# Expert retrieval in a two-layer trunk: second-table rows gathered per token and summed in four column groups, one tile behind the first table

## The reference

```python
top_s, pos = lax.top_k(cand, P_TOPK)
eidx = jnp.take_along_axis(cand_idx, pos, axis=-1)
gate = jax.nn.softmax(top_s, axis=-1).astype(xc.dtype)
u = jnp.take(u_tab, eidx, axis=0)
act = jax.nn.gelu(jnp.einsum('thkd,td->thk', u, xc))
vv = jnp.take(v_tab, eidx, axis=0)
return jnp.einsum('thk,thkd->td', gate * act, vv)
```

## Time and profile before

| what | us |
|---|---|
| median of 3 runs | 3196.29 (3189.86 to 3204.64) |
| span of the profiled execution | 3171.0 |
| until the first gather | 293 |
| tile 0 / 1 / 2 | 620 / 432 / 422 |
| tile 3 / 4 / 5 | 595 / 404 / 407 |

### The profile page before, as it was taken

The page is one execution under the profiler, slowest core; times in us unless marked ns, Lnnn a source line. Parts: engine busy times, 40 slices in busy tenths (PEclk is TensorE's granted clock), DMA queues, the critical chain, the costliest instruction groups (busy, mean ns, idle before and its releaser), DMA issues.

```text
span 3171.0 us, 27910 instructions
## 1 busy us (share of the span) xinstructions
PE 2487.3 (78%) x6500; PEld 1148.6 (36%) x6500; DVE 1897.5 (60%) x5815; ACT 550.0 (17%) x1600; POOL 1712.9 (54%) x1588
## 2 busy tenths in 40 slices
PE   7875888788979888767788896789966766666667
PEld 1244333345623233323354343444732222222222
DVE  0044367873475657768757538784366777477664
ACT  0121112222111111112211112332111111111111
POOL 0002445443366667667667544463346777577675
PEclk9867899888989989888889798888988888778888
DMA  8526787667889999989999787776768999789888
GB/s 293 198 94 239 282 285 275 236 241 266 300 319 401 402 403 401 368 299 343 359 378 396 247 307 255 262 285 223 274 222 323 360 351 337 293 325 339 320 327 303
DMA packets 298730, 961.85 MB, mean 303 GB/s; under 512 B 28304, under 2 KB 30736, under 8 KB 297840
## 3 DMA queue, kind: packets, MB, share of 16 engines
q0 software_dynamic: 221184, 805.40, 69.5%
q1 hardware_dynamic: 77328, 154.96, 13.6%
q10 hardware_dynamic: 96, 0.10, 0.0%
HBM read 957.63 MB, written 2.62 MB: 303 GB/s over the span
## 4 chain that ended last, share of the span: by engine, by line
PE 39%; DVE 29%; issue 14%; DMA 9%; POOL 3%; ACT 2%; another core or an unknown queue 2%; DVEq 0%; POOLq 0%; SPq 0%; ACTq 0%
PE ps_acc L785 17%; DVE u_ring L1309 10%; PE ps_mm L610 5%; PE ps_mm L751 5%; DMA u_ring<-peer_u,gathered 4%; PE ps_mm L571 3%; PE ps_mm L723 2%; DMA v_ring<-peer_v,gathered 2%; POOL u_ring L517 2%; DMA weights<-ada_w 2%; POOL v_ring L517 2%; PE ps_mm L664 1%; DVE half_idx L1262 1%; DVE half_top L1258 1%
## 5 line engine op out<-in xcount | busy, mean ns | idle before, releaser
L785 PE MATMUL ps_acc<-v_ring,diag 128*128 128x512 f32 x3072 | 1536.5, 654 | 452.4 <-ACT diag L979 249.0
L517 POOL DMA_INDIRECT u_ring<-peer_u,gathered x768 | 836.3, 1089 | 795.0 <-DVE dots L1309 466.9
L785 PEld LDWEIGHTS ps_acc<-v_ring,diag 128*128 128x128 f32 x3072 | 626.6, 211 | 1279.1 <-issue 1052.5
L517 POOL DMA_INDIRECT v_ring<-peer_v,gathered x768 | 861.3, 1121 | 339.8 <-issue 216.0
L1309 DVE CUSTOM_DVE_ANT_0 u_ring<-u_ring,h 128x1024 f32<-128x1024 f32 x768 | 908.3, 1221 | 71.9 <-DMA u_ring<-peer_u,gathered 68.3
L979 ACT ACTIVATE diag<-consts,coef 128x128 f32<-128x128 f32 x768 | 245.6, 390 | 150.3 <-DVE coef L1323 87.0
L610 PE MATMUL ps_mm<-weights,hT 128*128 128x512 f32 x480 | 213.4, 598 | 2.9 <-DMA weights<-w_in 1.8
L1321 DVE TENSOR_SCALAR gexp<-gexp 128x4 f32<-128x4 f32 x192 | 41.6, 217 | 282.3 <-ACT gexp L973 216.0
L973 ACT ACTIVATE gexp<-poly 128x4 f32<-128x4 f32 x192 | 39.3, 205 | 891.8 <-DVE poly L1318 658.3
L751 PE MATMUL ps_mm<-hT,weights 128*128 128x128 f32 (+1 forms) x1024 | 182.6, 332 | 9.2 <-issue 8.6
L571 PE MATMUL ps_mm<-weights,condT 128*2 128x512 f32 x384 | 172.4, 605 | 18.3 <-DMA weights<-ada_w 18.3
(11 more groups left out here) (184 smaller groups left out, 1820.4 us busy)
## 6 DMA issues: line engine op xcount, KB each, us to landing
weights<-ada_w SPq DMA_DIRECT2D x24, 2048.0 KB
weights<-w_in SPq DMA_DIRECT2D x20, 2048.0 KB
weights<-peer_wq SPq DMA_DIRECT2D x16, 2048.0 KB
weights<-w_out SPq DMA_DIRECT2D x8, 2048.0 KB
u_ring<-peer_u,gathered POOLq DMA_INDIRECT x768
v_ring<-peer_v,gathered POOLq DMA_INDIRECT x768
weights<-peer_keys SPq DMA_DIRECT2D x4, 1024.0 KB
par<-params SPq DMA_DIRECT2D x2, 1026.0 KB
```

The lines of the kernel that those rows point to most:

```text
L517: pool.indirect_dma_start(ring[:, slot, :], None, table, bass.IndirectOffsetOnAxis(ap=gathered[:, p, at:at + 1], axis=0)).then_inc(full[sl ...
L785: last = pe.matmul(ps_acc[:, b * NB:(b + 1) * NB], diag[:, slot, :], v_ring[:, slot, b * NB:(b + 1) * NB], start=False, stop=False)
```

## The change

**Second table by token.** A gather of the second table now fetches the 128 rows of one token: partitions are its picks. For this the picks (`picks`) and coefficients (`coef`) of a whole tile are transposed by PE (`turn`), copied by ACT (`copy_turned`), and POOL makes row numbers of them (`v_rows`). The sum over a token's picks is now the matmul's own sum over partitions. The stationary operand is a window of 32 columns that is zero but for one column, the token's coefficients (`coef_cols`, filled four times a tile by `spread` on ACT). Four tokens, one from each quarter of the tile, are taken together: their 32-column matmuls go to four column groups of the array and to four partition groups of `ps_acc`. That is 8 matmuls of 32 x 512 for four tokens, again 256 for a tile. The diagonals are gone.

**One tile behind.** Since a token's second-table rows are known only when all its picks are, the second table of a tile runs in a later stretch than the first. There are ten stretches (`segments`) in place of six tiles: first table of tile 0; second of 0; first of 1; first of 2 with second of 1; second of 2; first of 3; second of 3; first of 4; first of 5 with second of 4; second of 5. Where both tables are in a stretch, POOL takes one gather of each in turn, the second table 6 gathers behind. The dense parts are spread over the same groups of tiles as before, by `SPREADS`: 248 picks over two stretches for the first, 316 over three, 248 over two.

**Rings** are 6 buffers for the first table and 8 for the second; the second's are given back four at a time.

**Gelu and gates once per tile.** DVE makes the products of all 128 picks and then one set of gelu operations of 128 columns, with a tanh on ACT; the softmax gates are made once per tile as well. The copy of the scores ahead of ranking (line 1255) and the last operation of ranking on DVE (line 1296) are gone; adding the table's base is POOL's. At the start of a stretch two heads are ranked at once, and the other six in the middle of heads 0 to 5. No engine has a loop any more.

```diff
-URING = VRING = DRING = 2 * GROUP
+ITEMS = P_HEADS * TOPK
+URING, VRING = 6, 8
+QUADS = 4
...
+SPREADS = {(0, S_TILES): 2 * ITEMS - 8, (1, P_TILES): 2 * ITEMS + 60, (1, S_TILES): 2 * ITEMS - 8}
...
+            def gather_u(tau, i):
+                if i % TOPK == 0:
+                    take_head(tau, i // TOPK)
...
+                if n >= URING:
+                    pool.wait_ge(u_used, n - URING + 1)
...
+            def gather_v(tau, i):
+                if i == 0:
+                    pool.wait_ge(turned_ready, tau + 1)
...
+                if n >= VRING:
+                    pool.wait_ge(v_used, n - VRING + 1)
...
+            for g in segments():
+                ahead = URING if g.v is not None else 0
+                for i in range(ITEMS + ahead):
+                    if g.u is not None and i < ITEMS:
+                        gather_u(g.u, i)
+                    if g.v is not None and i >= ahead:
+                        gather_v(g.v, i - ahead)
...
+            def turn(tau):
+
+                pe.wait_ge(coef_ready, tau + 1)
                 if tau:
                     pe.wait_ge(x_fed, tau)
...
+                for k in range(QUADS):
+                    pe.wait_ge(v_full[(n + k) % VRING], ((n + k) // VRING + 1) * 16)
+                for b in range(2):
+                    for k in range(QUADS):
+                        t = token(i + k) % GROUPS
+                        at = (i % PART + k + 1) * GROUPS - 1 - t
+                        last = pe.matmul(ps_acc[GROUPS * k:GROUPS * (k + 1), b * NB:(b + 1) * NB],
+                                         coef_cols[:, i // PART % 2, at:at + GROUPS], v_ring[:, (n + k) % VRING, b * NB:(b + 1) * NB],
+                                         start=(t == 0), stop=(t == GROUPS - 1), tile_position=(0, GROUPS * k))
+                last.then_inc(v_used, QUADS)
...
-                step.before_search(dve.tensor_copy(st[:], peer_scores[:, where, :]))
...
+            def coefficients(tau):
+
+                dve.wait_ge(u_used, (tau + 1) * ITEMS)
+                step.after(dve.tensor_tensor(poly[:], dots[:], dots[:], ALU.mult))
+                step.after(dve.tensor_scalar(poly[:], poly[:], GELU_A, 1.0, ALU.mult, ALU.add))
+                dve.tensor_tensor(poly[:], poly[:], dots[:], ALU.mult).then_inc(poly_ready, 1)
...
+                for i in range(ITEMS):
+                    if to_feed and g.u is not None and i == (0 if g.beside == (1, S_TILES) else FEED_AT):
+                        feed(to_feed.pop())
+                    side.item()
+                    if g.u is None:
+                        continue
+                    if i % TOPK == TOPK // 2 and i // TOPK + AHEAD < P_HEADS:
+                        route(routed // P_HEADS, routed % P_HEADS)
+                        routed += 1
```

More of the change, by code:

```diff
@@ L137, with __init__, item @@
 class Beside:
-    def __init__(self, program, weight, steps, first=2):
-        self.program, self.weight, self.share = program, weight, weight / (GROUP * (steps - first - 2))
-        self.wait, self.due, self.done = first * GROUP, 0.0, 0
-    def quarter(self):
-        if self.wait:
-            self.wait -= 1
-            return
+    def __init__(self, program, weight, items):
+        self.program, self.weight, self.share = program, weight, weight / items
+        self.due, self.done = 0.0, 0
+    def item(self):
         self.due += self.share
@@ L151, in quarter @@
             self.done += next(self.program)
-    def step(self):
-        for _ in range(GROUP):
-            self.quarter()
     def end(self):
@@ L521, in head @@
-            def head(n, p, last=False):
-                for g in range(STEPS):
-                    if g + 1 < STEPS:
-                        gather(u_ring, u_full, u_used, peer_u, n, p, g + 1)
-                    elif not last:
-                        take(n + 1, 1 - p)
-                        gather(u_ring, u_full, u_used, peer_u, n + 1, 1 - p, 0)
-                    gather(v_ring, v_full, v_used, peer_v, n, p, g)
-            take(0, 0)
-            gather(u_ring, u_full, u_used, peer_u, 0, 0, 0)
@@ L809, in _ @@
                 pass
[L810 to L825 removed]
+            side, of = nothing(), None
+            for g in segments():
+                if g.beside != of:
+                    of = g.beside
+                    side = start_beside(of, modulate, dense_stages)
+                if g.v is not None:
+                    turn(g.v)
+                for i in range(ITEMS):
+                    side.item()
+                    if g.v is not None and i % QUADS == QUADS - 1:
+                        add_rows(g.v, i - QUADS + 1)
+                if g.v is not None:
+                    close_sum(g.v)
+                if g.last:
+                    side.end()
         @block.scalar
@@ L1327, in feed @@
+            def feed(tau):
                 t = tau % T
@@ L1383, in _ @@
-            feed(step, DEPTH * T - 1)
-PAIR_STEPS = 74
-QUARTERS_BEFORE_ROW = (2, 1, 1, 0)
-NEXT_STEPS = 62
+            side, of = nothing(), None
+            to_feed = []
+            routed = 0
+            for g in segments():
+                if g.beside != of:
+                    of = g.beside
+                    side = start_beside(of, modulate, dense_stages)
+                if g.u is not None:
+                    first = g.u * P_HEADS
+                    while routed < first + AHEAD:
+                        route(routed // P_HEADS, routed % P_HEADS)
+                        routed += 1
+                for i in range(ITEMS):
+                    if to_feed and g.u is not None and i == (0 if g.beside == (1, S_TILES) else FEED_AT):
+                        feed(to_feed.pop())
+                    side.item()
+                    if g.u is None:
+                        continue
+                    if i % TOPK == TOPK // 2 and i // TOPK + AHEAD < P_HEADS:
+                        route(routed // P_HEADS, routed % P_HEADS)
+                        routed += 1
+                    if i == GATE_AT:
+                        gate_diffs(g.u)
+                    if i == GATE_AT + 4:
+                        gates(g.u)
+                    dot(g.u, i)
+                if g.u is not None:
+                    coefficients(g.u)
+                if g.last:
+                    side.end()
+                if g.v is not None:
+                    to_feed.append(g.v)
+                    if g.u is not None or g.v == DEPTH * T - 1:
+                        feed(to_feed.pop())
```

394 lines of the change are left out of this document (166 added, 228 removed).

## The result

The changed kernel takes 3528.1 us (median of 4 runs, 3511.9 to 3533.9), the kernel before 3197.5 (3189.9 to 3204.6) beside it: 1.102 times as long, 95% interval 1.098 to 1.106. Forecast were 3109, in a range of 2960 to 3400. The sign was wrong, and the range too.

What follows compares the result with a forecast made beforehand. No engine full: PE nearly the bound in tiles 0 and 3, DMA in 1 and 2, POOL in 4 and 5. From 303, stretches, hand-overs and close summed to 3084, plus 25 gave 3109 us; range 2960 to 3400.

Steps and rivals of the forecast that it cites:

- I take half, 3.4: PE's eight matmuls for four tokens: 3.4 us, between 6.9 without overlap of column groups and 1.7 with all four overlapping.
- rival A: Second-table sum on PE: all four column groups overlap, four tokens take 1.7 us, whole kernel 2977 us; chance 0.17.
- Stretch kind 2: Second table alone, tiles 2 and 5: two fours of the ring take 11.1 us, the stretch 178.
- The hand-over, 8: Start of each second-table stretch: tanh, coefficients, transposes, copy, row numbers and first landing take 8 us, four times.
- Kind 4: Stretches gathering both tables: POOL's gathers set 389 us, 395 beside tile 2; PE and DVE have slack.
- 366: POOL's work in a stretch with both tables: 256 gathers at 1.43 us each, 366 us.
- Kind 1: First table alone: ranking, products and waits for POOL, 31.4 us a head; tiles 0, 1, 3, 4 at 290, 250, 280, 246.
- Kind 3: Second table with dense part, tiles 0 and 3: PE's 145 dense, 109 sum and 11 waits make 265 us.
- Rival C: First-table stretches wait for POOL, gathers beside products all taking 1.99 us: up to 282 us lost, halfway 3250; chance 0.12.
- Rival D: PE at the low clock in second-table-only stretches: a four takes 6.9 us, +56 twice, whole 3221 us; chance 0.08.
- Rival B: Second-table sum on PE: column groups don't overlap, a four takes 6.9 us, whole kernel 3452 us; chance 0.15.
- The median lies 25.3 above, so I add 25: Whole kernel: the profiled execution's span was 3171.0, the median 25.3 above, so 25 us were added to 3084.

Runs made afterwards that it cites:

- e4: Changed kernel, but PE waits for, sums and gives back each token's second-table row by itself, not in fours; 3386 us, ratio 1.060 to the kernel before.
- e6: Changed kernel, but the layer-1 prompt tile's dense part stands still where both tables are gathered; ratio 1.063 to the kernel before.
- e1: Changed kernel, but the layer-1 prompt tile's dense part spread over 120 items in place of 316, beside tile 1's first-table stretch; 3501 us, ratio 1.094.
- e5: Changed kernel, but all fourteen buffers serve the first table in the four stretches that gather from it alone; ratio 1.065 to the kernel before.
- e2: Changed kernel, but four idle first-table buffers serve as a third set of four in second-table-only stretches; 3405 us, ratio 1.064 to the kernel before.
- e7: Changed kernel, but PE makes four more matmuls of zeros behind every four of tiles 4 and 5; 3516 us, ratio 1.100 to the kernel before.

## Why the prediction was wrong, step by step

- **"I take half, 3.4" for a four.** Wrong mechanism, near value, by luck. The groups overlap fourfold (1.92 us at the high clock; rival A's 1.7), and at the low clock, where PE mostly was, a four is 3.4 to 3.6; the mean is 592/192 = 3.1. The Trainium skill ("TensorE: Matmul & The Clock Gate", part 3 on packing) has 2.38-fold for three column tiles; this trace shows close to 4 for four groups, where the prediction's scaling of that figure gives some 3.2. Even so rival A's time, 2977, did not come with its mechanism, since the sum was not the bound: e4 gave most of this overlap away and won 143 us.
- **Stretch kind 2, "lands 3.6 after that".** This step failed, 82 and 55 us; some 20 of the 82 are the dense part at V2's start (268 against V5's 248), which the forecast had at nothing. 3.6 is one row's bytes into an idle DMA. In the ring the last row of a four stands behind others: four rows are 5.2 us of bytes against 3.7 of issue, eight at a time, and 6.2 us pass. Two fours so take 14.4 us for the forecast's 11.1: 2.6 of the difference are landing, 0.2 the sum and 0.4 the signals. The trace of before would have told. A second-table gather and the matmul that waits for it, in tile 4 (POOL, then PE):

```profile
2459.64 1.99 POOL L517 DMA_INDIRECT v_ring<-peer_v,gathered  x1 [0.30 <-issue]
...
2466.20 1.12 PE L785 MATMUL ps_acc<-v_ring,diag 128*128 128x512 f32 x2 [3.90 <-DMA v_ring<-peer_v,gathered]
```

  6.56 us. The wait to be read is from the gather's start to the instruction that it frees, not to when its bytes have moved. The Trainium skill ("SBUF — State Buffer", the part on the DMA's set-up cost) puts about 2 us, mostly completion, on every transfer beyond its bytes; with 1.2 for one row at its 436 GB/s that makes 3.2, and the trace disagrees for rows in a queue. The hand-over, 8, was short too: in V5 the first sum starts 13 us after the turn, 10.4 of it from the first gather's start (3281.55), which is issue and landing of one four.
- **Kind 4, "PE and DVE have slack".** This step failed most, 167 us in U2 + V1. Busy shares of 27% and 44% are slack only if nobody waits in a circle. I priced the dense part by its work and asked only for the hand-over what is queued behind a wait. e6 shows that its place is the cause: out of that stretch the same work costs 63 us in place of 196; e1 that a place can be wrong in another way, 152. In U5 + V4, with no dense part, the miss is 35. The first gather starts 11 us into it, as "10.4" has it; the gathers then take 399 us, not 366. POOL's waits there (2860 to 3270 us) show 22 us for buffers behind the products, which "366" left out (the 16.9 are the wait before the first gather); whether that is the cause of the rest too was not tried:

```profile
POOL u_ring L536 <- DVE dots L1320: 22.1, 5, 7.6
POOL u_rows L524 <- DVE picks L1298: 16.9, 1, 16.9
```

- **Kind 1.** U4 came out at 250 for 246 and U0 at 300 for 290, U3 at 302 for 280; in U1 the forecast was 38 under. e5 shows that all four pay for the ring of six, 23 to 48 us, and U1 most. The forecast had only 2.6 us a head for it, 21 in a stretch. It came near in U4 by luck: DVE's work there is 200 us where the forecast has 225, and what is not work is 50 where it has 21. In U1 the bytes had the right price (240 us in e5), but the ring kept them from coming.
- **Kind 3** was 19 and 14 us under; e2 and e4 take that off again, so PE's work there was not alone the bound: the ring was as well. The sum's share of that work was less than the 109 of the forecast, 83 and 78 us.
- **Rival C** did not come: the mean of POOL's first-table gathers is 1.17 us, 1.47 with issue, under its turning point of 1.68. Its argument was misread, though. A gather that starts while a product runs takes about 0.94 us and what is left of that product: over the 412 such gathers of the kernel before it goes from 0.96 us, with under 0.2 left, to 1.96, with 1.0 to 1.2 left (four that start together with a product take 0.94). The 1.31 started 0.43 before the next product, the 1.99 1.09 before. So the 1.31 is no evidence against a block for the whole of a product. **Rival D** did in its clock (0.65 in V5) and not in its price, 18 us for one stretch in e7 against 56, because the groups overlap. **Rival B** gave 3452, the nearest time, for a reason that did not happen; by its own prices (98 us for each us of a four) it turns at 4.3 us a four, not 4.7.
- **"The median lies 25.3 above, so I add 25".** These 25 us do not lie around the span: the profiled run of the changed kernel took 3533.5 us with a span of 3531.7. They say only that the profiled execution of before was faster than the median run, and they don't change the forecast's ratio.
- **The frame.** "It can win where PE is tight" holds as far as it goes: V0 and V3, the stretches with most of PE's work, are the only second-table ones within 20 us of their forecast, and their tiles the only ones that got faster, by 15 and 6 us. But all rivals moved the price of an engine's work. None had the ring or a circle of waits as the bound, and these two decide.

## What to carry to other kernels

Splitting work into phases that use one resource each leaves the other phase's buffers idle; give them to the phase that runs, and price a phase by its ring's cycle (issue, start-to-use landing, use, return) before pricing it by any engine. In-order engines that each hold a piece of a side program can form a circle of waits: put the side program beside the phases with the fewest other links, and follow one waiting instruction all round. Relieving an engine is worth what the next bound allows: with all rings shared, tables apart and the ranking moved under the sums, the changed kernel beats the one before by 2.2 to 2.7%. When two variants come out the same, look whether they have the same bound before calling the difference worthless.

## What the runs showed of the hardware

- Two-pass fp32 matmuls of 32 output columns in four column groups run fully beside each other: 16 passes in 1.92 us at the high clock, where 16 x 0.43 is 6.9, and 3.4 to 3.6 at the low one. Token by token the same sum takes 1.45 us a token in V5 of e4, in place of 0.48 (1.92 / 4).
- A gather issued by POOL while DVE runs a product takes about 0.94 us and the rest of that product, 0.96 to 1.96 in all (kernel before, 412 gathers).
- Of 0.52 MB gathers issued 1.24 us apart behind a pause, the first has its bytes 3.7 to 4.0 us after its start, the fourth after 4.9 to 5.6, the eighth after 5.4 to 6.3 (changed kernel, 3280 to 3400 us).
- The same sum had a granted clock of 0.65 in V5 as fours (PE busy 112 of 254 us), 0.96 token by token in e4 (186 of 199), and 0.95 in e7 with matmuls of zeros between the fours (184 of 231).
- Two chips differed in the rate that they held for gathered rows, 357 against 409 GB/s over 100 us of the same code, and in the time of the kernel before, 3203 against 3092 us.
